# SSD rows of the output product as three f16 products, their weights split inside the solve; feed-forward copies moved behind the next split

## The reference

```python
y_ssd = _ssd_mixer(p_ssd, ...)             # 512 of the 1024 mixed features
y_rwkv = _rwkv7_mixer(p_rwkv, ...)         # the other 512
mix = jnp.concatenate([y_ssd, y_rwkv], axis=-1).astype(h.dtype) @ w_out[l]
h = h + _rms_norm(mix, post_mix_norm[l])
hn = _rms_norm(h, pre_ffn_norm[l])
u = _causal_dwconv(hn @ ffn_w_up[l], ffn_conv_w[l], ffn_conv_b[l])
gate, val = jnp.split(u, 2, axis=-1)
f = (jax.nn.silu(gate) * val) @ ffn_w_down[l]
h = h + _rms_norm(f, post_ffn_norm[l])
```

## Time and profile before

| | |
|---|---|
| median of 3 runs | 769.1 us (766.74 to 769.5) |
| the profiled execution, its own time | 765.5 us |
| its span in the profile | 763.7 us |
| PE / PEld busy | 741.5 / 603.2 us |
| DVE busy | 559.7 us |
| ACT busy | 423.1 us |
| POOL busy | 61.7 us |
| read from HBM | 127.35 MB |

### The profile page before, as it was taken

The page is one execution under the profiler, slowest core; times in us unless marked ns, Lnnn a source line. Parts: engine busy times, 40 slices in busy tenths (PEclk is TensorE's granted clock), DMA queues, the critical chain, the costliest instruction groups (busy, mean ns, idle before and its releaser), DMA issues.

```text
span 763.7 us, 16837 instructions
## 1 busy us (share of the span) xinstructions
PE 741.5 (97%) x7250; PEld 603.2 (79%) x7250; DVE 559.7 (73%) x906; ACT 423.1 (55%) x673; POOL 61.7 (8%) x104
## 2 busy tenths in 40 slices
PE   9999889889999999999999999999999999999997
PEld 7888777779868888888886777788878888865554
DVE  4799977663978999998666986899766576663443
ACT  6699452222664666667555763297554566653442
POOL 0000123030021011101002000002002000000000
PEclk9999989999999999999999999999999999999999
DMA  9990252111393456545791563338336065555101
GB/s 320 397 369 22 90 213 99 40 61 56 118 323 111 154 180 219 220 169 201 244 389 46 191 247 116 111 112 329 113 111 221 1 221 222 221 220 180 70 1 55
DMA packets 67145, 129.47 MB, mean 170 GB/s; under 512 B 3968, under 2 KB 28032, under 8 KB 66816
## 3 DMA queue, kind: packets, MB, share of 16 engines
q1 hardware_dynamic: 66032, 126.07, 45.4%
q0 software_dynamic: 320, 1.64, 0.6%
q10 hardware_dynamic: 720, 0.70, 0.3%
HBM read 127.35 MB, written 1.05 MB: 168 GB/s over the span
## 4 chain that ended last, share of the span: by engine, by line
PE 65%; DVE 20%; ACT 9%; DMA 3%; issue 2%; SPq 0%; DVEq 0%
PE bank L590 19%; PE bank L706 14%; PE bank L2971 11%; DVE arena L541 8%; DVE arena L2274 3%; PE bank L2361 3%; PE bank L1437 3%; DMA ring<-in_w_in_dram 3%; PE bank L809 2%; PE bank L700 2%; ACT arena L532 2%; PE bank L1456 1%; PE bank L2842 1%; PE bank L2823 1%; PE bank L1694 1%
## 5 line engine op out<-in xcount | busy, mean ns | idle before, releaser
L541 DVE SCALAR_TENSOR_TENSOR arena<-ring,arena 128x1024 f16<-128x1024 f32 x194 | 228.3, 1221 | 71.1 <-ACT arena L532 70.8
L590 PE MATMUL bank<-hg,arena 128*128 128x256 f16 x2496 | 276.1, 273 | 0.9 <-DVE arena L541 0.9
L590 PEld LDWEIGHTS bank<-hg,arena 128*128 128x128 f16 x2496 | 243.0, 98 | 33.3 <-issue 3.1
L532 ACT ACTIVATE arena<-ring 128x1024 f16<-128x1024 f32 x194 | 191.9, 1043 | 88.1 <-PE bank L2971 37.6
L2971 PE MATMUL bank<-arena 128*128 128x512 f16 (+1 forms) x480 | 83.6, 336 | 0.0
L2971 PEld LDWEIGHTS bank<-arena 128*128 128x128 f16 x480 | 47.0, 98 | 36.1
L706 PE MATMUL bank<-arena 128*128 128x256 f16 x528 | 58.2, 273 | 0.2 <-DVE arena L541 0.2
L706 PEld LDWEIGHTS bank<-arena 128*128 128x128 f16 x528 | 51.5, 98 | 6.8 <-issue 0.9
L706 PE MATMUL bank<-mix,arena 128*128 128x256 f16 x480 | 52.9, 273 | 0.0
L706 PEld LDWEIGHTS bank<-mix,arena 128*128 128x128 f16 x480 | 47.0, 98 | 5.7
L590 PE MATMUL bank<-xv,arena 128*128 128x256 f16 x336 | 37.4, 273 | 0.0
(11 more groups left out here) (404 smaller groups left out, 943.1 us busy)
## 6 DMA issues: line engine op xcount, KB each, us to landing
ring<-in_w_in_dram SPq DMA_DIRECT2D x12, 2048.0 KB, 9.9
ring<-in_ffn_w_up_dram SPq DMA_DIRECT2D x22, 1024.0 KB, 7.5
ring<-in_w_ff_dram SPq DMA_DIRECT2D x8, 2048.0 KB, 8.9
ring<-in_w_ff_dram SPq DMA_DIRECT2D x16, 1024.0 KB, 6.1
ring<-in_ffn_w_down_dram SPq DMA_DIRECT2D x11, 1024.0 KB, 6.1
ring<-in_w_out_dram SPq DMA_DIRECT2D x8, 1024.0 KB, 7.4
ring<-in_w_xk_dram SPq DMA_DIRECT2D x2, 2048.0 KB, 11.6
ring<-in_w_xv_dram SPq DMA_DIRECT2D x2, 2048.0 KB, 8.2
```

The source lines that it names most:

```text
L532: nc.scalar.activation(quarter(halves_of(chunk)[0], chunk, q), quarter(slot(*chunk), chunk, q), ACT.Copy, scale=W_SCALE).then_inc(*mark("w ...
L541: nc.vector.scalar_tensor_tensor(quarter(halves_of(chunk)[1], chunk, q), quarter(slot(*chunk), chunk, q), W_SCALE, quarter(halves_of(chunk ...
L590: mm = nc.tensor.matmul(out_, weight[a][:, k, cols], src[:, k, b, :], start=(first and i == 0), stop=(last and i == 2), skip_group_check=True)
```

## The change

The SSD rows become three f16 products like the rest. Their weights are split into free places: the halves of rows 0's quarters 0 and 1 go into `hg`, all others into ring slots of `w_out` itself, each over quarters that have been split already. So both slots are kept until the last bank of the product. The SSD output is written to another place (`YN`) and split from there into `mix16`. The splits stand inside the solve. In the feed-forward loop the f16 copies of a pair move behind the two splits and the tap of the next even bank.

```diff
-OUT1_AT = (10256, 11280, 9232, 12304)
...
+        def wout_quarter(i, q):
+
+            if i == 0 and q < 2:
+                return split_view(hg[:, 4 * q:4 * q + 4, :].rearrange("p k t -> p (k t)"))
+            rows, at_ = (0, q + 2) if i and q < 2 else (i, q - 2)
+            return split_view(slot("w_out", "rows", rows)[:, at_, :])
...
-                if q == 3:
-                    chunk_used("w_out", "rows", 1, ("out1 low", q))
...
-            split_rows = (0, 1) if name == "w_out_2" else (1,) if name == "w_out" else ()
+            split_rows = (0, 1) if name in ("w_out_2", "w_out") else ()
...
+                if name == "w_out" and tail:
+                    chunk_used(name, "rows", 0, used)
+                    chunk_used(name, "rows", 1, used)
...
+        def act_ssd_high(act):
+            act.wait_ge(*at("ssd out", 3))
+            for i in range(2):
+                nc.scalar.activation(mix16[:, 2 * i:2 * i + 2, 0, :], YN[:, 2 * i:2 * i + 2, :], ACT.Copy).then_inc(
+                    *mark("ssd_act", "ssd high", i))
...
@@ dve_rwkv_chunk
+            if c:
+                wout_low(dve, 0, (2, 3))
+            else:
+                wout_low(dve, 0, (0,))
             for g in range(2):
                 dve.wait_ge(*at("RB bank", c, g))
...
+            if c:
+                wout_low(dve, 1, (0, 1))
+                dve_ssd_low(dve)
             if c == 0:
+                wout_low(dve, 0, (1,))
@@ act_rwkv_chunk
+                wout_high(act, 0, (0, 1))
...
+                act_ssd_high(act)
                 act_y_scaled(act)
...
+            if c:
+                wout_high(act, 1, (0, 1))
             for g in range(2):
                 lo = 64 * g
                 act.wait_ge(*at("y bank", c, g))
...
+            wout_high(act, c, (2, 3))
@@ dve_rwkv_end
+            wout_low(dve, 1, (2, 3))
             dve_y_centre(dve, 1)
-            out1_low(dve, (0,))
...
@@ act_ffn
+                if b % 2:
+                    continue
+                if p:
+                    act_hidden(act, p - 1)
                 for i in range(2):
-                    if b % 2 == 0:
...
+                    act.wait_ge(*at("conv", 0, b, i))
```

79 lines of the change are left out of this document (42 added, 37 removed).

## The result

The changed kernel takes 776.72 us (median of 4 runs, 775.10 to 778.79) against 767.92 for the kernel before (4 runs, 766.3 to 769.5): a ratio of 1.0116, 95% interval 1.0086 to 1.0146. It is slower by 8.8 us. The forecast was 772.0 with a range to 775.2, and slower by over 0.5% had 0.34: the range and the likeliest case were both wrong. The profiled execution took 778.79 us with a span of 776.7; the one of before took 765.5 with 763.7.

The account below looks back on a forecast made before the run. PE, busy 97%, was taken to bound the kernel, with DVE setting the feed-forward loop's pace by a little. A loss of 5.1 less a gain of 2.2 made +2.9 us: 772.0 us on the median, range 767.3 to 775.2.

Parts of the forecast that it names:

- product, PE's two waits included: Output product on PE: f16 matmuls save 3.5 us, two waits for DVE take 3.0, some 0.4 us are left.
- held slots, at the start of the loop: Up 1, released only after the product, delays root and norm; the feed-forward loop starts 5.5 us later from the product's end.
- loop, until the down product: Feed-forward loop: DVE's pair falls from 10.82 to 9.9 us, under PE's 10.49, so 2.2 us are gained.
- ahead of the product: Solve before the output product: the other split quarters fit DVE's and ACT's idle time and cost nothing.
- The two waits: PE waits 1.6 us for keys 3 ahead of the product and 1.4 for the y chain before the second transposes.
- SP's wait for the last bank: Up 1 released at 212.4, landing 8.6 us later; ACT's root waits behind its high quarters, 7.7 us late.
- the loop's first scaling: DVE's first scaling in the feed-forward loop comes at 244.45 us instead of 237.57.
- the 5.1 of PE: Feed-forward loop: loss before its gain, PE's bank of up 2 at 250.7 us against 245.6.
- E: Rival: the feed-forward loop keeps 10.82 us a pair through a new DVE wait; sum +5.9, 775.0 us; chance 0.12.
- D: Rival: PE idles 3.9 us before the first feed-forward group and its clock drops; sum +4.6, 773.7 us; chance 0.15.

Follow-up runs that it names:

- e8: Kernel before, with only the release of both w_out slots held back to the last bank of the output product: 774.8 us, ratio 1.0095.
- e3: Changed kernel, with ACT making the root and the norm ahead of up 1's four high quarters: 767.58 us, ratio 1.0003 to the kernel before.
- e11: Changed kernel, with POOL's subtraction for the hidden low half cut to 8 of 256 columns: 772.29 us, ratio 1.0047 to the kernel before.
- e9: Changed kernel, with 30 matmuls of overwritten result filling most of PE's idle time before the first feed-forward group: 775.96 us, ratio 1.0105 to the kernel before.
- e4: Changed kernel, second solve: DVE makes SSD low halves and keys 3 before rows 1's low quarters, one later quarter behind the centring: 776.63 us, ratio 1.0108.
- e10: The changed kernel itself run once more: 777.54 us, ratio 1.0118 to the kernel before.
- e2: Changed kernel, with the feed-forward loop's ACT order (act_ffn) of before: 776.22 us, ratio 1.0103 to the kernel before.
- e6: e3 with DVE's second solve reordered: SSD low halves and keys before rows 1's low quarters, centring first: 764.95 us, ratio 0.9972 to the kernel before.
- e12: e9 with POOL's subtraction for the hidden low half cut to 8 of 256 columns: 771.22 us, ratio 1.0047 to the kernel before.
- e1: Kernel before, with only the changed order of the f16 copies in the feed-forward loop (act_ffn): 767.51 us, ratio 0.9999.
- e5: e1 with POOL's subtraction for the hidden low half cut to 8 of 256 columns: 765.92 us, ratio 0.9975 to the kernel before.
- e7: Kernel before, with ACT making the root and the norm ahead of up 1's four high quarters: 766.8 us, ratio 0.9985.

## Why the prediction was wrong

**The sum.** What the forecast had, and what the runs show in its place (the middle rows from the traces, counted between the same instructions of before and after):

| term | forecast us | measured us |
|---|---|---|
| product, PE's two waits included | -0.4 | -0.2 (27.97 against 28.20) |
| held slots, at the start of the loop | +5.5 | +6.6 on PE (28.59 against 21.98), +7.5 on DVE (32.43 against 24.91) |
| loop, until the down product | -2.2 | +1.1 on PE, so that +7.7 arrive (136.95 against 129.26) |
| ahead of the product | 0 | +5.5 in the one profile, about 1.3 in the medians |
| sum | +2.9 | +8.8 in the medians; +13.0 in the spans, whose four terms add up to it |

**What held.** The two waits, within 0.2 us of their size and on the releasers named. SP's wait for the last bank, ACT standing before the transfer with the root behind it: 8.36 us, and a root 8.2 late against the 7.7 forecast. Up 1 was usable 9.0 us after the product's end (227.11 - 218.12, where SP's issue follows at 218.14) where I took 8.6; the 6.8 estimated by the Trainium skill's formula (DMA: Bandwidth & Descriptors, Anatomy of one DMA) would have been further off. e8, which does this alone, and e3, which takes the root out from behind it and nothing else, show from both sides that it is the cause of the loss. For the loop's first scaling the forecast had 6.9 us of delay on DVE (244.45 - 237.57), which is 7.3 counted from the product's end; measured are 7.5 in the changed kernel and 7.6 in e8.

**The step that failed was the loop.** The forecast said "DVE needs 10.82 - 0.91 = 9.9 a pair": that subtraction holds only if every duration stays. I asked what DVE would wait for and not what ran inside its wait. POOL's subtraction did, so the pair came out at 10.84. The forecast even noted that POOL's low halves would come later, but asked only who reads them; they come 2.75 us later in the pair (273.74 - 270.78 against 258.16 - 257.95), and beside other instructions of DVE. Both errors of size follow from it. The 2.2 us did not come, and DVE's lateness did not melt: in the sum I had replaced its 6.9 by the 5.1 of PE, on the ground that PE would decide behind the first banks. It is DVE that decides throughout, and 7.6 us arrive. e11 shows the forecast's reasoning at work once POOL is out of the way: the loss falls by 2.9 of the 7.7.

**The rivals.** E, "The loop does not get faster", is what happened: the pace of 10.84 is its 10.82. Its mechanism, a new wait of DVE for ACT, is not there, and its sum of +5.9 was short by 1, since it too started from PE's 5.1. It had 0.12, the least but one, because I looked for a reason on ACT alone. D saw the hole (3.9 forecast, 4.09 measured) and the cold stretch behind it, but e9 shows its price at the end as zero while DVE is late: I had given it 0.45 us of slack behind DVE, and in fact all of its 1.1 to 1.4 us find room there. Behind a wait of 1.24 us at the transposes no low clock shows, but behind e4's 2.04 one does, and there it counts in full until the product's end. By that one profile D's mechanism has a price where PE itself is the last to be ready. (The range's upper end, 775.2, was called E's, whose own sum gives 775.0.)

**The rest is open.** 8.8 less 7.7 plus 0.2 leaves 1.3 us ahead of the product in the medians. The same reckoning, the difference in the medians less what the trace shows from L1895 on, leaves 1.4 or 1.5 in e10 and e2 and 0.7 in e4, but less than 0.4 either way in e3, e6, e9, e11 and e12, which have the same splits in the solve. So a delay ahead of the product that belongs to the change is not shown. In the profiles PE comes to L1895 at 185.1 to 190.0 us in the nine kernels with the split rows, and at 184.5 to 186.5 in the five without. Most of the spread arises in the second solve, from the turn of the first chunk (L2071 before) to the last stage of the blocks (L1799 before):

| kernels | us |
|---|---|
| without the split rows: before, e1, e5, e7, e8 | 18.41, 18.70, 17.63, 17.56, 17.86 |
| with them: changed, e10, e2, e3 | 22.25, 21.50, 21.60, 21.46 |
| with them: e4, e6, e9, e11, e12 | 18.37, 18.19, 18.34, 18.80, 18.44 |

The four in the second row have a second cold stretch there; in e10 it reads 0.55, 0.50, 0.50 and 0.74 of the full clock from 170 to 178 us:

```profile
172.00:174.00 2.00, 2.00 (x54) 1.54 (x54) 0.63 (x3) 1.09 (x4) 0.94 (x4) 0.50 1.09 386
```

e9, e11 and e12 run the same instructions up to there as the changed kernel and don't have it, so it comes in some executions and not in others. Four of nine with the split rows against none of five without may be the change or may be chance. It makes 3.8 (22.25 - 18.41) of the 5.5 us by which the profiled execution of the changed kernel is late at L1895, and so most of why that execution lies 13.3 us over that of before where the medians differ by 8.8. It was no step of the forecast.

## What to carry to other kernels

Before an engine's idle time is counted as gained, look at what the other engines do in it: one that shares its memory ports may have been working there for nothing. Where an engine sets the pace of a loop, its own lateness at the loop's start is the price of a delay, not that of the engine it feeds. Where a buffer is held longer, follow the transfer that waits for it to the first in-order instruction that needs it, and see what else stands behind that instruction: moving the root ahead of the high quarters returned 7.5 us by the trace, more than the 3.5 that the cheaper product had to give.

## What the runs showed of the hardware

- POOL's subtraction of 128x256 tiles lengthens DVE's two-input instructions beside it: four taps from 1.67 to 2.08 us, a low quarter from 1.22 to 1.69, 0.88 us for two tiles that take POOL 1.31 by themselves. On 8 columns it lengthens none (e5); its own second instruction then takes 1.46 us where the first takes 0.23, and ends with DVE's.
- Idle time of 4.09 to 4.17 us on TensorE brought a granted clock of 0.50 for about 6.8 us, of which some 5 were work; 30 dead matmuls in the hole kept it at 1.00. A wait of 2.04 us in the dense product of e4 was followed by 0.56 and 0.58 in the next 4 us.
- Such a stretch of 6.8 us cost the start of the down product nothing (e9) or 0.7 us (e12), by who was late beside it.
